# Latent-attention keys by pairs of heads, values in four units, and one weight copy moved behind the second attention step

## What is computed

```python
def mla_kv(ckv, kr, kv_norm_g, w_ukv, cos, sin):
    b, l = ckv.shape[:2]
    kv = (rms_norm(ckv, kv_norm_g) @ w_ukv).reshape(b, l, MLA_HEADS, MLA_NOPE + MLA_DV)
    if cos is not None:
        kr = apply_rope(kr, cos, sin)
    k_rope = jnp.broadcast_to(kr[:, :, None, :], (b, l, MLA_HEADS, MLA_ROPE))
    return jnp.concatenate([kv[..., :MLA_NOPE], k_rope], axis=-1), kv[..., MLA_NOPE:]
```

## Time and profile before

| | us |
|---|---|
| median of 3 runs | 2406.26 |
| lowest and highest of them | 2405.49, 2406.71 |
| the profiled execution, its own time | 2405.54 |
| its span, first to last instruction | 2403.6 |
| PE busy in it | 2299.0 (96%) |
| DVE, ACT, POOL busy | 1185.5, 860.2, 219.2 |
| mean granted clock of PE, as a share of full speed | 0.991 |

### The profile page before, as it was taken

One profiled execution on the slowest core, in us unless ns is written; L12 is line 12 of the kernel. 1 busy time (PEld: TensorE's weight loads), 2 busy tenths in 40 slices (PEclk: granted clock), 3 DMA queues, 4 the chain that ended last, 5 costly groups with the idle time before them and its releaser, 6 DMA issues.

```text
span 2403.6 us, 43295 instructions
## 1 busy us (share of the span) xinstructions
PE 2299.0 (96%) x19398; PEld 1834.1 (76%) x19398; DVE 1185.5 (49%) x1864; ACT 860.2 (36%) x1238; POOL 219.2 (9%) x204
## 2 busy tenths in 40 slices
PE   8999899989999999999999899889998999999998
PEld 5876598866658788888888587559874669888886
DVE  4674353259363551424244667435239455544454
ACT  5362233215454422221223536132323455322223
POOL 3013310000120100000000102411000120000000
PEclk9999999999999999999999999999999999999999
DMA  8227101233201121221211223611121302323231
GB/s 311 62 70 254 58 28 36 71 124 103 93 25 36 36 88 55 69 70 53 71 59 65 88 62 101 221 52 36 53 89 33 112 6 71 106 88 105 88 105 53
DMA packets 161119, 198.44 MB, mean 83 GB/s; under 512 B 18294, under 2 KB 129368, under 8 KB 160295
## 3 DMA queue, kind: packets, MB, share of 16 engines
q1 hardware_dynamic: 155536, 186.25, 24.1%
q10 hardware_dynamic: 4695, 9.05, 1.1%
q0 software_dynamic: 704, 0.37, 0.2%
HBM read 184.60 MB, written 11.06 MB: 81 GB/s over the span
## 4 chain that ended last, share of the span: by engine, by line
PE 85%; DVE 7%; ACT 4%; issue 3%; POOL 0%; DMA 0%; DVEq 0%; ACTq 0%
PE ps L1433 34%; PE ps L805 17%; PE ps L1367 4%; PE ps L1022 3%; PE ps L1311 2%; PE ps L839 2%; PE ps L783 2%; PE ps L898 2%; PE ps L1406 2%; PE ps L1160 1%; DVE region L2346 1%; PE ps L792 1%; PE ps L1324 1%; PE ps L1341 1%; PE ps L983 1%
## 5 line engine op out<-in xcount | busy, mean ns | idle before, releaser
L1433 PE MATMUL ps<-region_r 128*128 128x512 f32 (+1 forms) x1536 | 376.3, 353 | 0.0
L1433 PEld LDWEIGHTS ps<-region_r 128*128 128x128 f32 x1536 | 270.6, 188 | 40.9
L1433 PE MATMUL ps<-region_r,weights_r 128*128 128x512 f32 (+1 forms) x768 | 229.5, 353 | 0.0
L1998 DVE TENSOR_TENSOR weights_r<-weights,region_r 128x2048 fp32r<-128x2048 f32 x62 | 141.9, 2289 | 120.0 <-ACT region_r L1547 120.0
L1433 PE MATMUL ps<-mixed_r,weights_r 128*128 128x512 f32 (+1 forms) x672 | 200.9, 353 | 0.0
L1433 PE MATMUL ps<-modulated_r,region_r 128*128 128x256 f32 (+1 forms) x624 | 186.6, 353 | 0.0
L1433 PE MATMUL ps<-mixed_r,region_r 128*128 128x256 f32 (+1 forms) x624 | 186.5, 353 | 0.0
L1433 PEld LDWEIGHTS ps<-region_r,weights_r 128*128 128x128 f32 x768 | 144.3, 188 | 20.5
L1938 ACT ACTIVATE region<-ps,cst 128x768 f32<-128x768 f32 (+1 forms) x64 | 50.3, 797 | 299.6 <-PE ps L1433 281.6
L2497 DVE TENSOR_TENSOR region_r<-region 128x768 fp32r<-128x768 f32 (+1 forms) x64 | 52.8, 825 | 197.8 <-ACT region L1938 197.8
L1433 PEld LDWEIGHTS ps<-mixed_r,weights_r 128*128 128x128 f32 x672 | 126.3, 188 | 18.1
(11 more groups left out here) (400 smaller groups left out, 4731.7 us busy)
## 6 DMA issues: line engine op xcount, KB each, us to landing
weights<-in_w_mlp SPq DMA_DIRECT2D x64, 1024.0 KB, 5.6
weights<-in_w_ada SPq DMA_DIRECT2D x40, 1024.0 KB, 5.2
weights<-in_w_in SPq DMA_DIRECT2D x34, 1024.0 KB, 5.2
region<-in_w_ada SPq DMA_DIRECT2D x8, 1024.0 KB, 17.0
weights<-in_w_out SPq DMA_DIRECT2D x8, 1024.0 KB, 6.7
x_kept<-residual SPq DMA_DIRECT2D x2, 3072.0 KB, 12.4
region<-decays_kept ACTq DMA_DIRECT2D x4, 1536.0 KB, 11.4
residual<-x_kept SPq DMA_DIRECT2D x2, 3072.0 KB, 10.4
```

The source lines that it names most:

```text
L1433: last = mm(dst[:, CTX + a:CTX + b], w[:, k, m], r[:, a:b], start=(k == 0 and r is r_low), stop=(k == KB - 1 and w is low))
L1998: v.tensor_tensor(ring_r[:, at, :], ring[:, at, :], mlp_high(j), ALU.subtract).then_inc(w_low_ready, 1)
```

## The change

- The keys are made for two heads at a time: two products of 128 rows in place of four of 64. For that the load of `w_ukv` becomes two transfers, which put the key columns of all heads side by side in the first 256 columns of the slot and the value columns in the next 256. ACT still copies each head by itself.
- The values are still six products of 256 columns, but in four units: chunks 0 and 1, 2 and 3 share a bank and one copy, 4 and 5 have their own.
- In each layer the table of units is shorter by four, so the units behind it keep their banks.
- ACT's copy of the high part of the first quarter of the output weights moves from ahead of the first exponential to behind the copy of the second step's transposes (`i == 1`).

```diff
--- before.py
+++ after.py
@@ -46,8 +46,9 @@
     for _q in range(4):
         LOADS += [(_l, "mlp1", 4 * _q + _i) for _i in range(4)] + [(_l, "mlp2", 4 * _q + _i) for _i in range(4)]
 NSLOT = 3
-
-DMAS = {"ba": 4, "uq": 6}
+VT_CHUNKS = ((0, 1), (2, 3), (4,), (5,))
+
+DMAS = {"ba": 4, "uq": 6, "ukv": 2}
 
 
 def landed(n):
@@ -61,8 +62,8 @@
          + [("hf", i) for i in range(8)] + [("hi", i) for i in range(NC)]
          + [("hgate", i) for i in range(2)] + [("hrms", i) for i in range(2)]
          + [("ckv", 0), ("cq", 0), ("ckvsum", 0), ("cq", 1), ("cqsum", 0)]
-         + [("uk", i) for i in range(4)] + [("uq", i) for i in range(4)]
-         + [("vt", i) for i in range(NC)] + [("out", i) for i in range(KB)] + [("norm1", 0), ("norm2", 0)]
+         + [("uk", i) for i in range(2)] + [("uq", i) for i in range(4)]
+         + [("vt", i) for i in range(len(VT_CHUNKS))] + [("out", i) for i in range(KB)] + [("norm1", 0), ("norm2", 0)]
          + [(w, 8 * q + i) for q in range(4) for w in ("mlp1", "mlp2") for i in range(8)] + [("norm3", 0)])
 
 SQUARES = ([("norm0", i) for i in range(8)] + [("l2", i) for i in range(8)] + [("grms", i) for i in range(4)]
@@ -466,7 +467,7 @@
                 return ada_out, ADA_FIRST + i // 2 + 1
             last = {"ba": ("ba", 0), "qkv": ("qkv", 2 * i + 1), "gate": ("gate", 2 * i + 1), "hq": ("hq", 2 * i + 1),
                     "hf": ("hf", 2 * i + 1), "hi": ("hi", NC - 1), "hgate": ("hgate", 1), "cq": ("cq", 1), "ckv": ("ckv", 0),
-                    "uq": ("uq", 3), "ukv": ("vt", NC - 1), "out": ("out", 2 * i + 1), "mlp1": ("mlp1", 2 * i + 1),
+                    "uq": ("uq", 3), "ukv": ("vt", len(VT_CHUNKS) - 1), "out": ("out", 2 * i + 1), "mlp1": ("mlp1", 2 * i + 1),
                     "mlp2": ("mlp2", 2 * i + 1)}[what]
             return gemm_out, out_number(l, *last)
 
@@ -628,6 +629,10 @@
                             sp.dma_start(dst[:, k, :, 0:96], q[:, k]).then_inc(w_in_s[n % NSLOT], 16)
                             for e in range(2):
                                 sp.dma_start(dst[:, k, :, 96 + 16 * e:112 + 16 * e], q[:, k, :, 80 - 16 * e:96 - 16 * e]).then_inc(w_in_s[n % NSLOT], 16)
+                    elif what == "ukv":
+                        for e in range(2):
+                            sp.dma_start(ring[:, n % NSLOT, 256 * e:256 * e + 256].rearrange("p (h n) -> p h n", h=H),
+                                         src.rearrange("p (h e n) -> p e h n", h=H, e=2)[:, e]).then_inc(w_in_s[n % NSLOT], 16)
                     else:
                         sp.dma_start(ring[:, n % NSLOT, 0:ks * wide].rearrange("p (k n) -> p k n", k=ks),
                                      src.rearrange("(k p) n -> p k n", p=128)).then_inc(w_in_s[n % NSLOT], 16)
@@ -1281,22 +1286,26 @@
                 gemm_parts(l, "cq", 0, [1], p_high, p_low, lo)
                 sum_squares(l, "cqsum", 0, 2, ones, lo)
                 pe.wait_ge(cn_ready, 3 * l + 1)
-                w = arrived(l, "ukv")[:, 0:512].rearrange("p (k n) -> p k n", k=1)
-                for h in range(H):
-                    project(free_pair(l, "uk", h), w, CKV.unsqueeze(1), 1, 128 * h, 64).then_inc(gemm_out, 1)
+                ukv = arrived(l, "ukv")
+                for i in range(2):
+                    dst = free_pair(l, "uk", i)
+                    for a, b in streams(0):
+                        last = mm(dst[:, CTX + a:CTX + b], ukv[:, 128 * i:128 * i + 128], CKV[:, a:b], start=True, stop=True)
+                    last.then_inc(gemm_out, 1)
                 pe.wait_ge(cn_ready, 3 * l + 3)
                 w = arrived(l, "uq")[:, 0:1024].rearrange("p (k n) -> p k n", k=2)
                 for h in range(H):
                     last = project(free_pair(l, "uq", h), w, CQ, 2, 128 * h, 128, lo)
                     last.then_inc(gemm_out, 1)
-                wv = arrived(l, "ukv")[:, 0:512].rearrange("p (h n) -> p h n", h=H)
-                for ci in range(NC):
-                    dst = free_pair(l, "vt", ci)
-                    mm(dst[:, 512:768].rearrange("p (h n) -> p h n", h=H), CKV[:, 128 * ci:128 * ci + 128], wv[:, :, 64:128],
-                       start=True, stop=True).then_inc(gemm_out, 1)
+                for i, several in enumerate(VT_CHUNKS):
+                    dst = free_pair(l, "vt", i)
+                    for j, ci in enumerate(several):
+                        last = mm(dst[:, 512 + 256 * j:768 + 256 * j], CKV[:, 128 * ci:128 * ci + 128], ukv[:, 256:512],
+                                  start=True, stop=True)
+                    last.then_inc(gemm_out, 1)
                 pe.wait_ge(gemm_evac, number(UNITS, l, "out", 0) - 3)
                 hold_clock(pair(number(UNITS, l, "out", 0))[:, 512:1024], 1 + l)
-                pe.wait_ge(gemm_evac, number(UNITS, l, "vt", NC - 1) + 1)
+                pe.wait_ge(gemm_evac, number(UNITS, l, "vt", len(VT_CHUNKS) - 1) + 1)
                 pe.wait_ge(rope_done, 5 * (l + 1))
                 pe.wait_ge(kr_copied, l + 1)
                 steps = att_steps(l)
@@ -1864,15 +1873,17 @@
                 act.wait_ge(gemm_evac, number(UNITS, l, "cq", 1) + 1)
                 square(l, "cqsum", 1, CQ[:, 1, lo:], lo)
                 inverse_roots(l, [("cqsum", 0, 256, 2, lo)])
-                for h in range(H):
-                    copied(l, "uk", h, af(KH[0:64, h, :], tokens(finished(l, "uk", h))[0:64], ACT.Copy))
+                for i in range(2):
+                    keys = tokens(finished(l, "uk", i))
+                    af(KH[0:64, 2 * i, :], keys[0:64], ACT.Copy)
+                    copied(l, "uk", i, af(KH[0:64, 2 * i + 1, :], keys[64:128], ACT.Copy))
                 for h in range(H):
                     af(ROT[96:128, h, 0:SEQ], finished(l, "uq", h)[96:128, 512:1024], ACT.Copy)
                     copied(l, "uq", h, af(QH[0:96, h, lo:], tokens(pair(number(UNITS, l, "uq", h)), lo)[0:96], ACT.Copy))
-                for ci in range(NC):
-                    copied(l, "vt", ci, af(VT[:, ci, :], finished(l, "vt", ci)[:, 512:768], ACT.Copy))
+                for i, several in enumerate(VT_CHUNKS):
+                    n = len(several)
+                    copied(l, "vt", i, af(VT[:, several[0]:several[0] + n, :], finished(l, "vt", i)[:, 512:512 + 256 * n].rearrange("p (c e) -> p c e", c=n), ACT.Copy))
                 act.wait_ge(rope_done, 5 * (l + 1))
-                out_high_part(l, 0)
                 steps = att_steps(l)
 
                 def keys_of(i):
@@ -1904,6 +1915,8 @@
                     af(PT[i % 4][:, 0:keys_of(i)], t[:, CTX:CTX + keys_of(i)], ACT.Copy).then_inc(pt_ready, 1)
                     if i >= 2 and i % 2 == 0:
                         take_output(i // 2 - 1)
+                    if i == 1:
+                        out_high_part(l, 0)
                 take_output(len(steps) // 2 - 1)
 
                 act.wait_ge(pt_ready, ATT0[l + 1])
```

## The result

| | before | after |
|---|---|---|
| median, us | 2406.26 | 2413.54 |
| lowest to highest, us (7 runs each) | 2404.22 to 2408.09 | 2410.96 to 2422.46 |
| ratio after / before | | 1.0037, 95% interval 1.0025 to 1.0049 |
| the profiled execution, its span, us | 2405.54, 2403.6 | 2415.36, 2413.5 |

The kernel is slower: by 7.3 us between the medians, by 8.9 us (6.0 to 11.8) by the ratio, which goes by the means of the seven runs. The forecast was +3.2 us; the median lies 0.9 us above the range. The sign and the places of the waits are those of the forecast, the size is not. The lines of the kernel after are shifted: L792 is L797 (the keys' products have L1293 now), L1311 is L1320, L1341 is L1350, L1539 is L1548, L742 is L747, L755 is L760, L2425 to L2427 are L2438 to L2440, L2452 is L2465, L1367 (the first output product) is L1376.

The account below looks back on a forecast made before the run. PE was taken to bound the kernel, with 85% of the chain. The terms -1.3 - 0.5 + 2.8 + 2.2 = +3.2 us on the median 2406.26 gave 2409.5 us, range 2402.4 to 2412.6 us.

Parts of the forecast that it names:

- Keys: Keys' products ahead of the attention: made by pairs, they start it 1.3 us earlier in layer 0, 0.5 in layer 1.
- the hole ahead of its queries that was named as a sign: Layer 0, ahead of the queries: PE would show a hole of a microsecond after the change.
- The reason given for layer 1: Layer 1: DVE's rotations, moved up, meet POOL's four copies, are delayed 1.7 us and keep 0.5 of 2.2 us gain.
- The moved copy: Step 3, both layers: POOL's subtraction, released later, holds up DVE's scaling; transposes 2.8 us later in layer 0, 2.2 in layer 1.
- POOL's pairs in later steps: POOL's five other pairs would meet steps 4 to 10; price left as it was, bounded by 1.28 us a layer.
- rival 1: Clock falls behind step 3's new hole: 1.5 us more per layer, 2411.0 us in one, 2412.5 in both; chance 0.30.
- Rival 2: Step 3's collision costs nothing and layer 1's rotations run unhindered: -4.1 us, 2402.2 us; chance 0.22.
- rival 3: Keys aren't faster at all, since a query product waits for L2419 or a bank: 1.8 us more, 2411.3 us; chance 0.05.
- The load in two transfers and the values in four units: Ahead of the attention: the split `w_ukv` load and the fewer copies of values change nothing.
- that rule: Port lock of DVE and POOL, loser fully blocked: nothing hidden, keys' layer-1 gain 0, sum 0.5 us higher.

Follow-up runs that it names:

- e10: Kernel after, first output weights' subtraction on DVE, layer-1 key-row copies on ACT, `i == 11` for `i == 4` at program start; 2404.00 us, ratio 0.9985.
- e3: Kernel after with two more `hold_clock` products in step 3 of each layer, filling PE's hole; 2411.14 us, ratio 1.0023.
- e1: Kernel after with the output weights' copy back ahead of the first exponential, so keys, values and load alone changed; 2403.16 us, ratio 0.9995.
- e4: Kernel after with POOL's subtraction for the first output weights moved to DVE, plus `i == 11` for `i == 4` at program start; 2403.75 us, ratio 0.9993.
- e9: Kernel after with POOL's subtraction for the first output weights cut into four instructions of 512 columns; 2407.86 us, ratio 1.0000.
- e7: Kernel after, first output weights' subtraction on DVE, key-row copies on ACT in both layers, `i == 11` for `i == 4` at program start; 2404.14 us, ratio 0.9990.

## Why the prediction was wrong

**Keys: right.** -1.26 us measured in layer 0 (forecast -1.3) and -0.48 in layer 1 (forecast -0.5). In layer 0 PE has the hole ahead of its queries that was named as a sign, 1.36 us. The reason given for layer 1 shows in the timelines of DVE and POOL of the kernel after:

```profile
1915.07 1.34 DVE L2438 TENSOR_TENSOR region<-region 32x512 f32<-32x512 f32 x1 [0.85 <-ACT region L1882]
1916.44 1.19 DVE L2439 TENSOR_TENSOR region<-region 32x512 f32<-32x512 f32 x1
1917.67 1.19 DVE L2440 TENSOR_TENSOR region<-region 32x512 f32<-32x512 f32 x1
```

```profile
1914.28 4.04 POOL L747 COPY region<-region 32x768 f32<-32x768 f32 x4 [30.35 <-DVE region L2440]
```

The three rotations beside POOL's copies take 3.72 us in place of 3 x 0.69 = 2.07, a delay of 1.65 us where 1.7 was forecast, and POOL's four copies take 4.04 us in place of 3.12. In e10, without the copies beside them, the rotations take 0.69 us. The forecast let 2.3 us of copies go into DVE's row and had POOL keep its pace; in fact the two overlapped for 1918.32 - 1915.07 = 3.25 us and both were slowed. That the delay came out within 0.1 us is in part luck.

**The moved copy: right in place and, at step 3, in size.** In layer 0 the transposes of step 3 start at 675.82 against 669.80, +6.02 us, of which 661.47 - 658.23 = 3.24 us were there at the first scores: 2.78 us, forecast 2.8. In layer 1: 1943.82 - 1934.42 = 9.40, less 1925.42 - 1918.23 = 7.19: 2.21 us, forecast 2.2. In layer 1 another 0.54 us comes later, from POOL's pairs in later steps (the transposes at 1952.42 wait 0.62 us for a scaling that took 1.15 us on the chain); the forecast had left their price as it was. In layer 0 some 0.5 us is given back (2.3 us to the output product in e3), where the forecast gave nothing back. These two errors cancel: without falls the terms make -1.26 - 0.48 + 2.3 + 2.75 = +3.3 us against +3.2.

**The step that failed is the choice between the forecast and rival 1, and rival 1's price.** The forecast said of the hole "not every hole of that kind need have a fall behind it, and in layer 0 PE isn't full in those steps", gave it 0.30, and priced a fall at 1.5 us. The hole of layer 0 had a fall behind it in all three profiles that have it, and the two of after cost 72.35 - 69.90 = 2.4 and 74.23 - 69.90 = 4.3 us: the price was taken from the two windows of the earlier trace rows, which are worth 2 x (0.50 + 0.26) = 1.5 us of full clock; the windows of after from 674 to 684 are worth 2 x (0.06 + 3 x 0.50 + 0.15) = 3.4, and those of the second profile, from 668 to 680 alone, 6 x 2 x 0.50 = 6.0. The trace of before had a longer fall than the one that was taken for the price:

```profile
512.00:514.00 2.00, 2.00 (x102) 1.41 (x101) 1.85 (x4) 0.00 (x0) 0.00 (x0) 0.70 0.04 8
514.00:516.00 2.00, 1.03 (x54) 0.83 (x45) 1.92 (x4) 0.00 (x0) 0.00 (x0) 0.50 0.85 227
516.00:518.00 2.00, 2.00 (x8) 0.50 (x7) 0.42 (x1) 0.66 (x1) 0.00 (x0) 0.50 0.80 304
518.00:520.00 2.00, 1.83 (x117) 1.72 (x117) 0.88 (x2) 0.00 (x0) 0.00 (x0) 0.60 0.00 1
```

It is worth 2 x (0.30 + 0.50 + 0.50 + 0.40) = 3.4 us, as much as the one in after. The argument that PE isn't full in those steps of layer 0 didn't save it from a fall, nor from paying for it. Even rival 1 in both layers, 2412.5 us, lies under the median of 2413.54. The falls of layer 1 were not certain: none in the first profile, 60.41 - 56.33 = 4.1 us for two in the second.

**A hole that wasn't seen.** The forecast let PE gain 2.2 us in layer 1 while the rotations gain 0.5, and booked the difference at nothing. That difference shows as PE's idle 2.16 us ahead of the scores (0.23 before), and in 4 of 6 profiles a fall followed. In e1, e4 and e9, which have that fall and none in step 3, the stage is 0.8 to 2.2 us longer than before (in e9 partly for a scaling); in e7 and e10, without the hole, 0.1 us. A gain that PE can't use isn't free where idle time can cost clock.

**How it adds up.** Over the runs of the experiments, the spans of before (74) average 2404.7 us at a mean granted clock of 0.9923, those of after (12, with the first seven) 2412.8 us at 0.9883. At equal clock:

| mean granted clock | before, us (runs) | after, us (runs) |
|---|---|---|
| 0.989 | 2408.3 (8) | 2411.9 (3) |
| 0.990 | 2408.5 (5) | 2411.0 (1) |
| 0.991 | 2406.7 (13) | 2409.1 (1) |
| 0.992 | 2404.2 (12) | 2408.9 (1) |

After is 2.4 to 4.7 us longer there, 3.4 on the mean of the six runs, about the forecast's +3.2 for the waits. A line through each kernel's runs with one slope for all gives 1.18 us for 0.001 of clock: the 0.0040 by which the clock is lower make 4.7 us. Together that is the 8.1 us between the means. This is an accounting, not a proof of each part: by the same line the keys alone gain 3.6 us where their stages show 1.7, and the move alone loses 6.8 where its stages without falls show 2.3 + 2.75 = 5.1. What makes those 1.7 to 1.9 us is open.

Where the clock is lost can be read from the profiles. Summed over windows of 2 us, time x (1 - clock) makes, within the span, 22.1 and 20.6 us in the two profiles of before, none of it in the attention stages of the table, and 27.6 and 28.5 us in those of after, of which 3.4 and 11.9 us lie in these stages. What is lost elsewhere, 24.2 and 16.5 us, is on the mean no more than before. So in these four profiles the clock that after has less lies in the falls behind its new holes. The stages of the two profiles are longer by 5.8 and 11.7 us, 8.8 on the mean, where the ratio of the runs has 8.9; with two profiles so far apart that is close by luck.

**The other rivals.** Rival 2 (the collision costs nothing) is refuted by the scaling of 4.04 us; rival 3 (keys not faster) by 18.39 against 19.65. The load in two transfers and the values in four units were booked at nothing, and e1 bears that out.

**On the port.** That DVE's scaling stands still until POOL's instruction ends is shown by e9: 4.04 us beside one instruction of 4.49, 0.81 beside quarters. The Trainium skill ("SBUF — State Buffer", section "SBUF: two separate sides") says that the pair of ports which DVE and GpSimd share goes to whichever starts first for the whole instruction while the other fully blocks. The 4.04 and 0.81 us agree. By the letter of that rule the forecast had the layer-1 gain of the keys at 0; it was 0.48 us.

## What to carry to other kernels

Moving a cheap copy also moves the work that it releases on other engines: look up what waits for it, what that work blocks, and whether the new place has a cover. Price every new idle stretch of the matrix engine twice, by its length and by the clock that may be lost behind it, and take that second price from the longest fall in the trace, not the shortest. Where a long POOL instruction shuts DVE out, cut it into pieces or give it to DVE at a slack moment; both took the 4 us scaling away here. And let an experiment change one thing: e4, e7 and e10 each differ at the start of the program too, which their question doesn't need, and so their kernel times can't be read cleanly.

## What had not been expected

- A hole of 2.16 us was followed by a fall of the clock in 4 of 6 profiles, and one of 2.72 us in 3 of 3.
- Two profiles of the same kernel differ by 4.1 us (before) and 7.6 us (after) at the first key of layer 0, 640 us into the run. Summed as above, the two of before lost the same 15.4 us of clock up to there, so the clock alone doesn't explain their 4.1 us. Offsets of that size ahead of a change say nothing of the change; stages cut around it do.
- In layer 0 the clock behind the same hole was at 0.50 for three windows of 2 us in one profile and for six in another of the same kernel, a difference of 1.9 us in the stage.
